# A layer chain on one core: the first mixer's order of products, the PSUM banks of its tail, and its row spreads

## What is computed

```python
z = rmsnorm(h, mix_norm) @ w_in          # split into hq, hf, hi, hg, cq, ckv, kr
o_a = hgrn2_mixer(hq, hf, hi, hg, ...)   # gated linear recurrence, 4 heads of 128
o_b = mla_mixer(cq, ckv, kr, ...)        # latent attention, 4 heads, 128 + 64 wide
mix = concatenate([o_a, o_b]) @ w_out
# hgrn2_chunk_scan, per chunk: o = (q exp(b)) S + tril(q k^T decay) v
#   S = exp(b_last) S + (k exp(b_last - b))^T v
# mla_mixer: q = rope(rmsnorm(q_up)); k = rope(rmsnorm([k_nope, kr]))
#   softmax(q k^T * scale, masked by chunk) v
# then: h = h + mix; h = h + relu(rmsnorm(h) @ up)^2 @ down; second layer, second block
```

## Time and profile before

| | us |
|---|---|
| runs shown | 1321.48, 1321.53, 1323.66 |
| median | 1321.53 |
| profiled execution | 1322.67 |
| its span, first to last instruction | 1320.9 |
| TensorE busy | 1274.9 |
| VectorE busy | 897.8 |
| ScalarE busy | 742.6 |

### The profile page before, as it was taken

The page is one execution under the profiler, slowest core; times in us unless marked ns, Lnnn a source line. Parts: engine busy times, 40 slices in busy tenths (PEclk is TensorE's granted clock), DMA queues, the critical chain, the costliest instruction groups (busy, mean ns, idle before and its releaser), DMA issues.

```text
span 1320.9 us, 24695 instructions
## 1 busy us (share of the span) xinstructions
PE 1274.9 (97%) x10319; PEld 1246.0 (94%) x10319; DVE 897.8 (68%) x1549; ACT 742.6 (56%) x1263; POOL 6.4 (0%) x16
## 2 busy tenths in 40 slices
PE   5989989999999999999999999999999989999997
PEld 5977769999999999999999999999999889999997
DVE  4884357666444776544675799974787747999655
ACT  5764145566444666433455666664766856666644
POOL 1000000000000000000000000000000000000000
PEclk9998869999999999999999999999999989999998
DMA  6222006554555265556365366665255334666640
GB/s 251 81 76 85 32 1 223 176 175 163 191 169 169 91 224 182 188 183 192 128 218 169 125 198 195 186 212 180 97 172 181 112 112 144 194 193 196 201 128 33
DMA packets 58891, 205.54 MB, mean 156 GB/s; under 512 B 6515, under 2 KB 8860, under 8 KB 58524
## 3 DMA queue, kind: packets, MB, share of 16 engines
q1 hardware_dynamic: 57104, 201.77, 47.3%
q10 hardware_dynamic: 1676, 2.19, 0.6%
HBM read 202.87 MB, written 1.06 MB: 154 GB/s over the span
## 4 chain that ended last, share of the span: by engine, by line
PE 90%; ACT 4%; DVE 4%; issue 1%; DMA 0%; ACTq 0%; DVEq 0%
PE PS L361 70%; PE PS L409 7%; PE PS L372 2%; PE PS L443 2%; PE PS L392 1%; DVE WL L346 1%; PE PS L623 1%; PE PS L2250 1%; ACT WH L339 1%; PE PS L490 1%; ACT EE L2408 1%; PE PS L727 0%; PE PS L729 0%; ACT L502 0%; PE PS L2317 0%
## 5 line engine op out<-in xcount | busy, mean ns | idle before, releaser
L346 DVE TENSOR_TENSOR WL<-RAW,WH 128x1024 fp32r<-128x1024 f32 (+2 forms) x385 | 460.8, 1202 | 224.4 <-ACT WH L339 223.7
L339 ACT ACTIVATE WH<-RAW 128x1024 fp32r<-128x1024 f32 (+2 forms) x385 | 392.3, 1038 | 234.8 <-PE PS L361 201.3
L361 PE MATMUL PS<-UH,WH 128*128 128x256 f32 (+2 forms) x1576 | 449.2, 285 | 8.9 <-DVE WL L346 4.9
L361 PE MATMUL PS<-UH,WL 128*128 128x256 f32 (+2 forms) x1576 | 448.9, 285 | 0.0
L361 PE MATMUL PS<-UL,WH 128*128 128x256 f32 (+2 forms) x1576 | 448.7, 285 | 0.0
L361 PEld LDWEIGHTS PS<-UH,WH 128*128 128x128 f32 (+1 forms) x1576 | 299.7, 190 | 9.9 <-ACT M L1695 4.2
L361 PEld LDWEIGHTS PS<-UH,WL 128*128 128x128 f32 (+1 forms) x1576 | 299.9, 190 | 0.0
L361 PEld LDWEIGHTS PS<-UL,WH 128*128 128x128 f32 (+1 forms) x1576 | 298.4, 189 | 0.0
L361 PE MATMUL PS<-HL,WH 128*128 128x272 f32 (+1 forms) x512 | 145.8, 285 | 0.0
L361 PE MATMUL PS<-HH,WH 128*128 128x272 f32 (+1 forms) x512 | 145.7, 285 | 0.0
L361 PE MATMUL PS<-HH,WL 128*128 128x272 f32 (+1 forms) x512 | 145.4, 284 | 0.0
(11 more groups left out here) (390 smaller groups left out, 1959.4 us busy)
## 6 DMA issues: line engine op xcount, KB each, us to landing
RAW<-wpack SPq DMA_DIRECT2D x363, 512.0 KB, 4.2
RAW<-wpack SPq DMA_DIRECT2D x16, 384.0 KB, 3.6
RAW<-wpack SPq DMA_DIRECT2D x6, 256.0 KB, 2.7
X<-xin SPq DMA_DIRECT2D x1, 1088.0 KB, 4.9
C<-cst SPq DMA_DIRECT2D x1, 1072.0 KB, 10.0
HB<-bias_rows ACTq DMA_DIRECT2D x1, 1024.0 KB, 5.7
out<-X SPq DMA_DIRECT2D x4, 256.0 KB, 2.3
VF<-cst ACTq DMA_DIRECT2D x1, 512.0 KB, 3.9
```

Of the source, the lines that this page charges most:

```text
L339: a.e.activation(WH[n % NH][:, 0:w], RAW[n % NR][:, 0:w], ACT.Copy).then_inc(*a.mark("wh", n))
L346: v.e.tensor_tensor(WL[n % NH][:, 0:w], RAW[n % NR][:, 0:w], WH[n % NH][:, 0:w].bitcast(f32), ALU.subtract).then_inc(*v.mark("wl", n))
L361: ins = t.e.matmul(o, part(n, hw, kw, a, b), x(kx), start=first and not i and not p, stop=last and i == len(kcs) - 1 and p == 2)
```

## The change

- `root_spread` and `spread_columns` use 128 rows for block 0 too (the identity's further rows are zero in its 16 columns).
- `values` is called once per token block. The order on TensorE becomes: query sums, value group, turned keys, value group, key sums, value group, query rotation, value group, key rotation, value group, spread for the keys, value group, chunks. ScalarE evacuates in that order. `rotate` takes as many banks as it fills.
- Around the levels ScalarE does `queries` ahead of the table load and of level 4's exponents, and `query_rest` ahead of level 5's; VectorE does `query_rest` ahead of level 4's operands and mask copy. VectorE's key roots come one split earlier.
- The tail's banks are numbers: the filler's 0, the output 4 to 7, scores of block 2 in 0 to 3, out sums 4, scores of block 1 in 5, 6, 7, 0, scores of block 0 in one bank, 1, head by head, hg 2 and 3 in 2 and 3, `out_rows` 4 to 7; `turn` goes on at 0. The two fillers ahead of the output are gone. The order becomes scores 2, out sums, scores 1, scores 0.
- ScalarE takes the root of the out sums ahead of the exponentials; VectorE inverts it between the scores of block 2 and block 1.

```diff
+    def go_on(self, b):
+        self.n += (b - self.n) % 8
...
-                n = z - a
-                ins = t.e.matmul(PS[:, b, a:z], rooted(st, x, n).to_broadcast([n, 128]), ID[0:n, 0:n], start=True, stop=True)
+                ins = t.e.matmul(PS[:, b, a:z], rooted(st, x).to_broadcast([128, 128]), ID[:, 0:z - a], start=True, stop=True)
...
+            def project(key, js, freed, bs=()):
...
+                    b = banks.put(t, bs[i], (key, j), (freed, key, j)) if bs else banks.take(t, (key, j), (freed, key, j))
...
+            def values(uu, i):
                 n = unit_at["hi", 2 * uu]
+                a, z = TILES[i]
+                b = banks.take(t, ("hi", uu, i), ("vt", uu, i))
+                products_rows(t, PS[0:z - a, b, 0:256], halves_of(n), 256, lambda k: UH[:, k, a:z],
+                              lambda k: UL[:, k, a:z], u_ready).then_inc(*t.mark("mix", "hi", uu, i))
+                if i == 2:
+                    for x in range(2):
+                        sig.also(("used", n + x), ("mix", "hi", uu, 2))
+            def keys_turned():
                 for i, (a, z) in enumerate(TILES):
-                    b = banks.take(t, ("hi", uu, i), ("vt", uu, i))
-                    products_rows(t, PS[0:z - a, b, 0:256], halves_of(n), 256, lambda k: UH[:, k, a:z],
-                                  lambda k: UL[:, k, a:z], u_ready).then_inc(*t.mark("mix", "hi", uu, i))
-                for x in range(2):
-                    sig.also(("used", n + x), ("mix", "hi", uu, 2))
+                    t.wait_ge("kdec")
+                    b = banks.take(t, ("kt", i), ("kt", i))
+                    for hh in range(4):
+                        ins = t.e.transpose(PS[0:z - a, b, 128 * hh:128 * hh + 128], KD[:, hh, a:z], ID[:, :])
+                    ins.then_inc(*t.mark("mix", "kt", i))
...
-                        ins = t.e.matmul(PS[:, b + hh, a:z], col(i, hh, z - a).to_broadcast([z - a, 128]),
-                                         ID[0:z - a, 0:z - a], start=True, stop=True)
+                        ins = t.e.matmul(PS[:, b + hh, a:z], col(i, hh).to_broadcast([128, 128]), ID[:, 0:z - a],
+                                         start=True, stop=True)
...
-                b = banks.take(t, ("hs", "o"), ("hroot", "o"))
+                b = banks.put(t, 4, ("hs", "o"), ("hroot", "o"))
...
-                b = banks.take(t, ("hr", "o"), ("onorm",), 4)
+                b = banks.put(t, 4, ("hr", "o"), ("onorm",), 4)
...
-                b = banks.take(t, ("rot", key), ("rsin", key), 4)
+                b = banks.take(t, ("rot", key), ("rsin", key), nh)
...
+            def scores(i, bs):
                 a, z = TILES[i]
-                n = z - a
-                b = banks.take(t, ("sc", i), ("sc", i), 4)
                 t.wait_ge("rsum", "q")
                 t.wait_ge("rope", "k")
                 for hh in range(4):
-                    t.e.matmul(PS[0:n, b + hh, 0:z], QN[:, hh, a:z], KN[:, hh, 0:z], start=True, stop=False)
+                    banks.put(t, bs[hh], ("sc", i, hh), ("sc", i))
+                    t.e.matmul(PS[:, bs[hh], 0:z], QN[:, hh, a:z], KN[:, hh, 0:z], start=True, stop=False)
                 for hh in range(4):
-                    ins = t.e.matmul(PS[0:n, b + hh, 0:z], QR[:, hh, a:z], KRR[:, hh, 0:z], start=False, stop=True)
+                    ins = t.e.matmul(PS[:, bs[hh], 0:z], QR[:, hh, a:z], KRR[:, hh, 0:z], start=False, stop=True)
                 ins.then_inc(*t.mark("mix", "sc", i))
+            def scores_in_front(b):
+                banks.put(t, b, ("sc", 0), ("sc", 0))
+                for hh in range(4):
+                    o = PS[0:16, b, 16 * hh:16 * hh + 16]
+                    t.e.matmul(o, QN[:, hh, 0:16], KN[:, hh, 0:16], start=True, stop=False)
+                    ins = t.e.matmul(o, QR[:, hh, 0:16], KRR[:, hh, 0:16], start=False, stop=True)
+                ins.then_inc(*t.mark("mix", "sc", 0))
...
-            spread_columns("l", lambda i, hh, n: LAT[0:n, 1, i:i + 1], ("rkv",), 1)
+            spread_columns("l", lambda i, hh: LAT[:, 1, i:i + 1], ("rkv",), 1)
             up("kvup", 0, [(0, 2), (1, 3)], 128, ("kn",))
             level(4)
             value_up()
             level(5)
             head_sums_by_token("q", QSQ, ("qm",))
-            values(0)
+            values(0, 0)
+            keys_turned()
+            values(0, 1)
             head_sums_by_token("k", KSQ, ("hroot", "k"))
+            values(0, 2)
             rotate("q", QR, 4)
+            values(1, 0)
             rotate("k", KR, 1)
-            for i, (a, z) in enumerate(TILES):
-                t.wait_ge("kdec")
-                b = banks.take(t, ("kt", i), ("kt", i))
-                for hh in range(4):
-                    ins = t.e.transpose(PS[0:z - a, b, 128 * hh:128 * hh + 128], KD[:, hh, a:z], ID[:, :])
-                ins.then_inc(*t.mark("mix", "kt", i))
-            values(1)
-            spread_columns("k", lambda i, hh, n: KSC[0:n, i, hh:hh + 1], ("rope", "k"), 4)
+            values(1, 1)
+            spread_columns("k", lambda i, hh: KSC[:, i, hh:hh + 1], ("rope", "k"), 4)
+            values(1, 2)
             for ch in range(4):
                 chunk(ch)
             project("hg", range(2), "ev")
-            keep_going(t, 2)
-            ob = banks.take(t, ("out",), ("outa",), 4)
+            banks.put(t, 0, ("ones",), None)
+            ob = banks.put(t, 4, ("out",), ("outa",), 4)
...
-            scores(2)
-            scores(1)
+            scores(2, range(4))
             out_sums()
-            scores(0)
-            project("hg", range(2, 4), "ev")
+            scores(1, (5, 6, 7, 0))
+            scores_in_front(1)
+            project("hg", range(2, 4), "ev", (2, 3))
             out_rows()
+            banks.go_on(0)
...
@@ scalar_mixer @@
+            queries()
             preload(a, ACT.Exp)
             exponents(4)
-            queries()
             act_split(a, 17)
+            query_rest()
             exponents(5)
-            query_rest()
             a.wait_ge("mix", "hr", "l")
             a.e.activation(RKV, PS[:, banks.at["hr", "l"], 0:T], ACT.Copy).then_inc(*a.mark("rkv"))
             act_split(a, 19)
...
             act_split(a, 22)
-            values(0)
+            values(0, 0)
+            for i, (p0, z) in enumerate(TILES):
+                a.wait_ge("mix", "kt", i)
+                a.e.activation(KT[0:z - p0, i, :], PS[0:z - p0, banks.at["kt", i], :], ACT.Copy).then_inc(*a.mark("kt", i))
+            values(0, 1)
             act_split(a, 23)
             a.wait_ge("mix", "hs", "k")
             a.e.activation(KSC[:, :, :], PS[:, banks.at["hs", "k"], 0:12].rearrange("p (i h) -> p i h", h=4), ACT.Sqrt,
                            bias=EPS[:, 0:1], scale=1.0 / 192).then_inc(*a.mark("hroot", "k"))
-            for i, (p0, z) in enumerate(TILES):
-                a.wait_ge("mix", "kt", i)
-                a.e.activation(KT[0:z - p0, i, :], PS[0:z - p0, banks.at["kt", i], :], ACT.Copy).then_inc(*a.mark("kt", i))
+            values(0, 2)
             act_split(a, 25)
-            values(1)
+            values(1, 0)
+            values(1, 1)
+            values(1, 2)
...
+            a.wait_ge("mix", "hs", "o")
+            a.e.activation(ROOTO, PS[:, banks.at["hs", "o"], 0:T], ACT.Sqrt, bias=EPS[:, 0:1], scale=1.0 / 128).then_inc(
+                *a.mark("hroot", "o"))
             preload(a, ACT.Exp)
...
-            a.wait_ge("mix", "hs", "o")
-            a.e.activation(ROOTO, PS[:, banks.at["hs", "o"], 0:T], ACT.Sqrt, bias=EPS[:, 0:1], scale=1.0 / 128).then_inc(
-                *a.mark("hroot", "o"))
...
@@ vector_mixer @@
             dve_split(v, 16)
+            query_rest()
             operands(4)
             attention(4)
-            query_rest()
...
+            dve_split(v, 22)
+            key_roots()
             dve_split(v, 23)
-            key_roots()
...
+            def probabilities(i):
+                _, P, _, sm = block(i)
                 v.wait_ge("pexp", i)
                 v.e.reciprocal(sm, sm).then_inc(*v.mark("psum", i))
                 v.wait_ge("psum", i)
                 for hh in range(4):
                     ins = v.e.tensor_scalar(P[:, hh, :], P[:, hh, :], sm[:, hh:hh + 1], None, ALU.mult)
                 ins.then_inc(*v.mark("p", i))
+            scores(2)
             v.wait_ge("hroot", "o")
             v.e.reciprocal(ROOTO, ROOTO).then_inc(*v.mark("hrec", "o"))
+            scores(1)
+            scores(0)
+            for i in (2, 1, 0):
+                probabilities(i)
```

More of the change, by code:

```diff
@@ L843, in exponents, with values @@
                 a.e.activation(ee[:, :, rng], ee[:, :, rng], ACT.Exp).then_inc(*a.mark("exp", i))
-            def values(uu):
-                for i, (p0, z) in enumerate(TILES):
-                    m = z - p0
-                    a.wait_ge("mix", "hi", uu, i)
-                    a.wait_ge("rr", "m")
```

(25 more changed lines are left out.)

10 lines of the change are left out of this document (1 added, 9 removed).

## The result

| | changed kernel, us | kernel before, us |
|---|---|---|
| runs | 1301.29, 1301.63, 1302.9, 1307.4 | 1317.81, 1321.48, 1321.53, 1323.66 |
| median | 1302.27 | 1321.51 |
| profiled execution | 1301.63 (span 1299.8, clock 0.984) | 1322.67 (span 1320.9, clock 0.973) |

The ratio is 0.9865, 95% interval 0.9831 to 0.9899. The forecast of 1303.0 is 0.7 us off. The sum behind it is not that good. Up to the second root spread it missed by 4.4 us, 3.2 of them in the term of the new order, and 4.4 us that it did not have came in far behind the change. That the two cancel is luck.

The account below looks back on a forecast made before the run. TensorE was taken as the bound, so only its waits and slow-clock time in the first mixer could be won. Terms -0.6, -3.5, -6.2, +0.35, -9.8 sum to -19.75 from 1322.67: 1302.9, rounded to 1303.0 us, range 1299.0 to 1308.5.

Parts of the forecast that it names:

- new order: Query sums to gates: reordered values, turns, sums and rotations take 32.9 us at full clock against 39.06, -6.2 us.
- Root spreads: Two root spreads with a 16-token block: 128 rows throughout make six records 0.3 us shorter in each, -0.6 us.
- Queues: ScalarE and VectorE around the levels: earlier query copies and query rest let the query sums start earlier, -3.5 us.
- rival A: New order: the clock falls once to three times more than taken, time 1304.5 to 1307.5 us; chance 0.15.
- Banks of the output: Output products: bank 4 was the second gate's, so they wait for its evacuation, less filler removed, +0.35 us.
- Tail: Scores to first attend: wait for L1307 goes and pieces run at full clock, 30.29 becomes 20.4 us, -9.8 us.
- B: Tail: scores stay at 1.2 GHz although the wait is gone, time 1312.5 us; chance 0.06.
- C: Tail: ScalarE's table loads, root and exponents bound it, not TensorE, time 1305 us; chance 0.05.
- Nothing behind 240 us is touched.: Rest of the kernel after the first mixer: claimed unchanged, with no term in the sum.
- Rival D: Spreads: 128 rows do nothing, +1.8 us, time 1304.5 us; chance 0.04.
- E: New order: clock falls at the first sums and stays low until the gate projections, time 1335.1 us; chance 0.02.

## Why the prediction was right in time, step by step

- **Root spreads, -0.6.** Measured 0.11 and 0.23, together -0.3. The price of the first was the second's, and the first's records are slow whatever their rows: 1.66 us for six of 128 rows, 0.28 each at full clock, where the second's took 0.12. Undoing the spreads gave 3.84, 1.77 and 0.96 back. By the rule of the Trainium skill ("TensorE: Matmul & The Clock Gate", "LDWEIGHTS (loading the stationary operand)") that a load of few rows takes as long as a full one, nothing would have changed. The trace doesn't agree, and it was right to go by its rows.
- **Queues, -3.5.** Measured -4.1, and -3.3 in the second profile; 4.3 and 3.5 on undoing it. Mechanism and bounds held. The working took the key products at 4.58 us, as slow as before; in the first profile they ran at full clock and took 3.3, and 0.7 of these 1.3 us were lost again at the value products (0.5 in a wait for their weights).
- **New order, -6.2. This step failed.** Measured -3.0, of which 1.16 are the key spread's and the order has -0.2 to 1.3. The sum took all pieces at full clock on the argument that it hadn't fallen behind the query sums before. The mechanism of rival A came instead, with two falls, though not its time, and the value group behind each was 1.55 and 1.4 us longer than one of 2.83: that is 2.95 of the 3.1 us by which 36.03 is over the 32.9 of the working. The turned keys, which rival A counted as a further source of falls, brought none in this profile. The gain of 1.8 us for the rotation's banks was counted as if the wait lay at full clock. It lay in a half-clock stretch that begins behind the key sums anyway, where it costs 0.9 us by an estimate that takes the stretch's length as given (it stands in for 1.8 us of work at half speed); and the new order paid 1.1 us in new waits. The version with the wait back was no slower.
- **Banks of the output, +0.35.** Measured +0.35.
- **Tail, -9.8.** Measured -10.35: scores, out sums and gates at the pieces' forecast lengths but for the front's, 1.14 us for 1.6 (the added changes between 128 and 64 rows cost 0.09 each), and 4.4 us from the last gate product to the first attend. Rivals B and C fell. What the working did not see is that the starting value was one execution's: the other profile of the kernel before had 24.4 us there, so the part is worth 4.5 to 10.35. The forecast of the time hardly hangs on it, since the start moves too: from the other profile, 1317.58 and -4.0 for the tail, the same sum gives 1303.6.
- **"Nothing behind 240 us is touched." This failed by -5.7 us.** The diff sets the count of a shared allocator, and a count that differs at the end of the changed part changes all that follows. One line in the kernel before gave 4.4 us of it.
- The sum up to the second root spread missed by 4.4 us (-15.4 for -19.75), and the bank count made up for it. The forecast was right in time by that luck. No run gives the order more than 1.3 of its 6.2 us.
- Rival D is out by the spreads undone, E by the clock being back at 1.00 at 100.8 and 111.0.

Not tried: the root of the output alone in its old place, and the banks of the tail undone alone. What decides where a half-clock stretch begins and how long it lasts stays open: the same kernel had it at 97 and 108 us in one execution and at 84 and 97 in another.

## What to carry to other kernels

Take a second profile of the kernel before, before a term is built on one stretch's clock: 17 us at half clock in a stage was 3.4 in the next execution. When a change moves a rotating allocator's count (here the number from which `Banks.take` goes on), write down what it is at the end of the changed part and compare it with that of before, since every later reuse moves with it; a sweep over that one number is worth a run each. Ask of a wait that you remove whether it lies inside a half-clock stretch, and set the new waits against it: 1.8 us of wait went here and the time stayed. Where an engine idles 1 to 3 us ahead of small matmuls at half clock, work that fills the idle time can be worth more than the removal of a wait elsewhere: here some 5 us for 40 unused products.

## What was not expected of the hardware

- Spread records with one row count throughout were faster than mixed ones, 2.68 us for 24 against 3.84, and 0.73 against 0.96 for six, although 128 rows are more work than 16. The front's sixteen score records in the tail point the same way: 0.60 us with eight of 128 rows and then eight of 64, 1.14 with the two in turn. What the array does in between wasn't taken apart.
- In 11 of the 13 profiles with whole sums (24 matmuls of one column, 2.57 us) a fall to 1.2 GHz begins during one of the two batches or within 2 us behind it (13 of the 26 batches); in halves of 12, in the one profile of that, it doesn't. That the batches cause it is not shown.
- Filler products held the attends at 2.4 GHz: 10.7 us for 15.95.
